# A two-layer hybrid decoder step on one core: the first layer's gate after its norm, mixers in another order, and half of the experts' down pieces in fp16 halves

## What is computed

```python
for i in range(DEPTH):                                  # 2 layers
    n = rms_norm(h, norm_mix[i])
    z = n @ w_in[i]                                      # 1024 -> 7 x 1024
    xa, ya, xb, g_post, g_pre, m_a, m_b = jnp.split(z, SPLIT_IDX, axis=-1)
    ua, ca_new = causal_dwconv(xa, ca0[i], conv_a_w[i])  # width 4
    ua = ua + conv_a_b[i]
    ha, h_last = rg_lru(ua, ...)                         # gated scan
    out_a = (ha * jax.nn.gelu(ya)) @ w_a_out[i]
    ub, cb_new = causal_dwconv(g_pre * xb, cb0[i], conv_b_w[i])
    out_b = (g_post * ub) @ w_b_out[i]
    merged = jax.nn.sigmoid(m_a) * out_a + jax.nn.sigmoid(m_b) * out_b
    h = h + merged @ w_o[i]
    n2 = rms_norm(h, norm_ffn[i])
    h = h + (swiglu(n2, ...) if i == 0 else moe_swiglu(n2, ...))   # top 2 of 8
    h = h + jax.nn.sigmoid(rms_norm(h, norm_ple[i]) @ w_ple_gate[i]) * (p[i] @ w_ple_proj[i])
return rms_norm(h, final_norm), ...
```

## Time and profile before

| what | value |
|---|---|
| median of 3 runs | 1177.38 us (1176.94 to 1178.35) |
| the profiled execution's own time | 1176.44 us |
| its span, and mean granted TensorE clock | 1174.8 us, 0.995 |
| read from HBM | 286.53 MB, 245 GB/s over the span |

### The profile page before, as it was taken

One profiled execution on the slowest core, in us unless ns is written; L12 is line 12 of the kernel. 1 busy time (PEld: TensorE's weight loads), 2 busy tenths in 40 slices (PEclk: granted clock), 3 DMA queues, 4 the chain that ended last, 5 costly groups with the idle time before them and its releaser, 6 DMA issues.

```text
span 1174.8 us, 27209 instructions
## 1 busy us (share of the span) xinstructions
PE 1139.4 (97%) x11871; PEld 919.3 (78%) x11871; DVE 872.5 (74%) x975; ACT 651.7 (55%) x681; POOL 26.8 (2%) x60
## 2 busy tenths in 40 slices
PE   7899999999999999889999998999999999999996
PEld 5788888888888888778888885877777777776565
DVE  5996896779766667896988677977676676767455
ACT  5575644466545457576564446855465555555252
POOL 4000001000000001000001000000000000000000
PEclk9999999999999999999999999999999999999998
DMA  9665566555665654356566654999999999998601
GB/s 284 198 226 180 187 209 215 181 186 171 218 211 181 212 183 143 127 187 223 177 227 228 218 214 178 401 408 396 380 392 382 375 386 379 397 388 320 245 1 39
DMA packets 171069, 289.33 MB, mean 246 GB/s; under 512 B 5195, under 2 KB 132187, under 8 KB 170954
## 3 DMA queue, kind: packets, MB, share of 16 engines
q1 hardware_dynamic: 169040, 283.20, 67.7%
q0 software_dynamic: 1728, 4.16, 1.3%
q10 hardware_dynamic: 202, 0.51, 0.2%
HBM read 286.53 MB, written 1.52 MB: 245 GB/s over the span
## 4 chain that ended last, share of the span: by engine, by line
PE 88%; DVE 7%; ACT 3%; issue 1%; DMA 1%; ACTq 0%; SPq 0%; DVEq 0%
PE acc L572 15%; PE acc L574 15%; PE acc L573 15%; PE aux L916 12%; PE acc L902 5%; PE acc L901 5%; PE acc L903 5%; PE aux L937 2%; PE acc L558 1%; PE acc L564 1%; PE acc L557 1%; PE aux L846 1%; DVE wl L1596 1%; PE aux L750 1%; PE aux L729 1%
## 5 line engine op out<-in xcount | busy, mean ns | idle before, releaser
L1596 DVE SCALAR_TENSOR_TENSOR wl<-raw,wh 128x2048 f16<-128x2048 f32 x124 | 283.3, 2288 | 87.0 <-ACT wh L1092 86.6
L572 PE MATMUL acc<-xn,wh 128*128 128x264 f16 x1184 | 326.8, 276 | 7.6 <-ACT xa L1136 5.0
L574 PE MATMUL acc<-xn,wl 128*128 128x264 f16 x1184 | 326.8, 276 | 0.0
L573 PE MATMUL acc<-xn,wh 128*128 128x264 f16 x1184 | 326.8, 276 | 0.0
L1092 ACT ACTIVATE wh<-raw 128x2048 f16<-128x2048 f32 x124 | 235.6, 1902 | 2.2 <-DMA raw<-in_w_in 2.2
L902 PE MATMUL acc<-ga,wh 128*128 128x96 f16 x1536 | 199.4, 206 | 1.3 <-issue 1.3
L901 PE MATMUL acc<-ga,wh 128*128 128x96 f16 x1536 | 199.4, 206 | 0.0
L903 PE MATMUL acc<-ga,wl 128*128 128x96 f16 x1536 | 199.4, 206 | 0.0
L1602 DVE SCALAR_TENSOR_TENSOR wl<-raw,wh 128x2048 f16<-128x2048 f32 x64 | 144.2, 2287 | 59.4 <-ACT wh L1101 59.4
L1101 ACT ACTIVATE wh<-raw 128x2048 f16<-128x2048 f32 x64 | 121.9, 1910 | 100.1 <-PE acc L903 96.3
L902 PEld LDWEIGHTS acc<-ga,wh 128*128 128x128 f16 x1536 | 150.3, 98 | 7.8 <-issue 7.6
(11 more groups left out here) (334 smaller groups left out, 1807.1 us busy)
## 6 DMA issues: line engine op xcount, KB each, us to landing
raw<-in_moe_w_gu SPq DMA_DIRECT2D x64, 1024.0 KB, 10.0
raw<-in_w_in SPq DMA_DIRECT2D x56, 1024.0 KB, 5.1
raw<-in_ffn_w_gu SPq DMA_DIRECT2D x24, 1024.0 KB, 5.3
sa<-in_moe_w_gu SPq DMA_DIRECT2D x16, 1024.0 KB, 9.3
xb<-in_moe_w_gu SPq DMA_DIRECT2D x16, 1024.0 KB, 10.7
raw<-in_ffn_w_dn SPq DMA_DIRECT2D x12, 1024.0 KB, 4.9
ya<-in_moe_w_dn SPq DMA_DIRECT2D x10, 1024.0 KB, 7.5
sg<-in_moe_w_dn SPq DMA_DIRECT2D x10, 1024.0 KB, 7.5
```

Of the source, the lines that this page charges most:

```text
L572: nc.tensor.matmul(bank, hi, x[:, 0, x0 + k, :], start=(k == 0), stop=False)
L573: nc.tensor.matmul(bank, hi, x[:, 1, x0 + k, :], start=False, stop=False)
L574: last = nc.tensor.matmul(bank, lo, x[:, 0, x0 + k, :], start=False, stop=(k == k_chunks - 1))
L1596: op(V.scalar_tensor_tensor(out=wl[:, s, 0:size], in0=raw_slot[s][:, 0:size], scalar=WS, in1=wh[:, s, 0:size], op0=ALU.mult, op1=ALU.subtr ...
```

## The change

1. **Down pieces.** For experts 0 to 6, pieces 1, 3 and 5 (21 of 48) are split like other weights: ScalarE rounds the loaded piece into `dn_h` (`hi_dn`), VectorE writes the remainder (`lo_dn`), both in `side`, the buffer of the block-diagonal gate weights, which has room for one piece. VectorE also splits two chunks of `hid_e` into `hid_h` (two operations). TensorE makes 12 fp16 matmuls of 512 columns in place of 4 in fp32. The loads that reuse such a piece's slot wait for `dn_lo`. The scale moves into `csr`. The embedding projection's weights of layer 1 go into `side` too, and are loaded by POOL only after the last split piece.
2. **Gate of layer 0** (`ple_mid`). It is a matrix on the normalised `xn`: TensorE sums the squares (four matmuls), projects, then multiplies; ScalarE takes the tanh out of PSUM. The gate of layer 1 (`ple_end`) stays early. All early matrices use `ga`.
3. **Mixers.** The last early unit's remainder of mixer 0 goes behind the four steps of 1/rms; ScalarE evacuates units 2 and 3 ahead of taps and roundings; the convolution of unit u-1 stands behind the scaling of unit u; one operation of the GELU is dropped into the next and into the scale of the tanh.

The core of the diff:

```diff
@@ -43,6 +43,9 @@
+SPLIT_DN = (1, 3, 5)
+
 IN_SECTIONS = 7
...
@@ -191,6 +195,18 @@
         spill_g, spill_t, spill_u, spill_w = (w1_flat[:, at + i * CAP:at + (i + 1) * CAP] for i in range(4))
+        hid_h = w1_flat[:, at:at + 2 * EC // 2 * CAP // 2].bitcast(F16).rearrange("p (s c t) -> p s c t", s=2, c=EC // 2)
+        dn_h = side[:].rearrange("p a c n -> p (a c n)").bitcast(F16).rearrange("p (s n) -> p s n", s=2)
+        def split_down(i):
+            e, g = i // DN_U, i % DN_U
+            return e < NE - 1 and g in SPLIT_DN
...
@@ -341,6 +358,8 @@
                     sp.wait_ge(g_lo, GU_ALL)
+                elif split_down(i - D_SLOTS):
+                    sp.wait_ge(dn_lo, splits(i - D_SLOTS) + 1)
                 else:
...
@@ -490,6 +515,8 @@
             nc.gpsimd.memset(nt[:, :, 2, :], 0.0).then_inc(nt_clear, 1)
+            pool.wait_ge(dn_mm, (NE - 1) * DN_U)
+            project_weights(LAYERS - 1)
             pool.wait_ge(aux_done, AX_POS)
...
-            def ple(l, n, done=0):
-                projected(l, range(done, C))
-                early_stats()
-                if l:
-                    pe.wait_ge(sc_done, C)
-                early_matrix(n, HX_PLE[l], before_norm=True)
             mixer(0)
-            early_matrix(N_GU, HX_FFN, early_stats)
+            early_matrix(N_GU, 1, early_stats)
             pe.wait_ge(xn_ready, 4 * 2)
...
                     unit(N_DN + SEC * k + u, u, u % 2, hid, C, 256, x0=C * k, at=at, last_unit=k == 2 and u == SEC - 1)
-            ple(0, N_PLE[0])
+            norm_stats()
+            projected(0, range(C))
+            matrix(N_PLE[0], xn, xn_ready, 4 * 2, before_norm=True)
...
@@ -906,16 +926,28 @@
                 e, g = i // DN_U, i % DN_U
-                pe.wait_ge(d_loaded[i % D_SLOTS], 16 * (i // D_SLOTS + 1))
-                pe.wait_ge(hid_e_ready, BLOCKS * e + g // 2 + 1)
+                split = split_down(i)
+                if split:
+                    pe.wait_ge(dn_lo, splits(i) + 1)
+                    pe.wait_ge(hid_h_ready, splits(i) + 1)
+                    th, tl = (dn_h[:, s, :].rearrange("p (c m) -> p c m", c=2) for s in range(2))
+                else:
+                    pe.wait_ge(d_loaded[i % D_SLOTS], 16 * (i // D_SLOTS + 1))
+                    pe.wait_ge(hid_e_ready, BLOCKS * e + g // 2 + 1)
+                    w = down_slot(i).rearrange("p (c m) -> p c m", c=2)
                 if g == 0 and e:
                     pe.wait_ge(ys_ready, 2 * e)
-                w = down_slot(i).rearrange("p (c m) -> p c m", c=2)
                 end = g == DN_U - 1
                 for half, k in [(h, k) for h in range(2) for k in range(2)] if end else [(h, k) for k in range(2) for h in range(2)]:
-                    last = nc.tensor.matmul(aux[0:CAP, 2 + half, :], hid_e[:, 2 * g + k, :],
-                                            w[:, k, half * 512:(half + 1) * 512], start=(2 * g + k == 0),
-                                            stop=(2 * g + k == EC - 1))
+                    bank, ms = aux[0:CAP, 2 + half, :], slice(half * 512, (half + 1) * 512)
+                    first, stop = 2 * g + k == 0, 2 * g + k == EC - 1
+                    if split:
+                        x = hid_h[:, :, g // 2 * 2 + k, :]
+                        nc.tensor.matmul(bank, x[:, 0, :], th[:, k, ms], start=first, stop=False)
+                        nc.tensor.matmul(bank, x[:, 0, :], tl[:, k, ms], start=False, stop=False)
+                        last = nc.tensor.matmul(bank, x[:, 1, :], th[:, k, ms], start=False, stop=stop)
+                    else:
+                        last = nc.tensor.matmul(bank, hid_e[:, 2 * g + k, :], w[:, k, ms], start=first, stop=stop)
                     if end and half == 0 and k == 1:
...
@@ -1099,6 +1134,14 @@
                 nc.scalar.activation(wh[:, j % SLOTS, :], g_slot[j % G_SLOTS], ACT.Copy, scale=WS).then_inc(g_hi, 1)
+            def hi_dn(i):
+                act.wait_ge(d_loaded[i % D_SLOTS], 16 * (i // D_SLOTS + 1))
+                k = splits(i)
+                if k:
+                    act.wait_ge(dn_mm, max(j for j in range(i) if split_down(j)) + 1)
+                nc.scalar.activation(dn_h[:, 0, :], d_slot[i % D_SLOTS], ACT.Copy, scale=WS).then_inc(dn_hi, 1)
...
@@ -1259,17 +1300,19 @@
                         hi(n0 + LEAD)
+                    elif u < 2:
+                        hi(n0 + u + LEAD)
+                        if u == l == 1:
+                            stats()
+                        evac(n0 + u, xa[:, 2 * u:2 * u + 2, 3:3 + T])
+                        if u == 1:
+                            norm_hi()
+                            act.wait_ge(aux_done, AX_VEC)
                     else:
+                        evac(n0 + u, xa[:, 2 * u:2 * u + 2, 3:3 + T])
+                        first_tap(u - 2)
                         hi(n0 + u + LEAD)
-                    if u == l == 1:
-                        stats()
-                    if u > 0 or l:
-                        evac(n0 + u, xa[:, 2 * u:2 * u + 2, 3:3 + T])
-                    if u == 1:
-                        norm_hi()
-                        act.wait_ge(aux_done, AX_VEC)
-                    if u:
-                        first_tap(u - 1)
+                first_tap(SEC - 2)
                 if l == 0:
...
-            def ple(l, n):
+            def ple_mid(n):
+                stats()
+                projected(range(4))
+                norm_hi()
+                projected(range(4, C))
+                for u in range(SEC):
+                    hi(n + u + LEAD)
+                    if u:
+                        early_pair(u - 1, 1, False)
+                    if u == SEC - 1:
+                        early_last(n + u, 1, False, ACT.Tanh, 0.5 * UNSCALE)
+                    else:
+                        evac_ot(n + u, ACT.Tanh, 0.5 * UNSCALE)
+            def ple_end(n):
...
@@ -1504,6 +1549,8 @@
                         by_token(e + 2)
+                    if e >= 0 and split_down(e * DN_U + g + 1):
+                        hi_dn(e * DN_U + g + 1)
                     if e == NE - 1 and g in (2, 3, 4):
...
@@ -1602,6 +1649,12 @@
+            def lo_dn(i):
+                vec_e.wait_ge(dn_hi, splits(i) + 1)
+                op(V.scalar_tensor_tensor(out=dn_h[:, 1, :], in0=d_slot[i % D_SLOTS], scalar=WS, in1=dn_h[:, 0, :],
+                                          op0=ALU.mult, op1=ALU.subtract), dn_lo)
...
@@ -1814,8 +1863,10 @@
                     lambdas()
-                lo(n0 + LEAD)
-                norm(v("norm_mix", l))
+                    norm(v("norm_mix", l), scaled=lambda: lo(n0 + LEAD))
+                else:
+                    lo(n0 + LEAD)
+                    norm(v("norm_mix", l))
@@ -1823,18 +1874,21 @@
                     op(V.tensor_tensor(xa[:, s, 3:3 + T], xa[:, s, 3:3 + T], by_rstd(), ALU.mult), xa_scaled)
+                    if u:
+                        vec_e.wait_ge(tap_ready, SEC * l + u)
+                        conv(ua, xa, 4, row, bias, u - 1)
                     lo(n + u + 1 + LEAD)
-                    vec_e.wait_ge(tap_ready, SEC * l + u + 1)
-                    conv(ua, xa, 4, row, bias, u)
                 n += SEC
...
                     evacuated(n + u)
-                    op(V.tensor_scalar(gx[:, s, :], gx[:, s, :], 0.044715 * GELU_C, GELU_C, ALU.mult, ALU.add))
-                    settle()
-                    op(V.tensor_tensor(gx[:, s, :], gx[:, s, :], ya[:, s, :], ALU.mult), vec_step if u == SEC - 1 else dv)
+                    op(V.scalar_tensor_tensor(out=gx[:, s, :], in0=gx[:, s, :], scalar=1.0 / GELU_A, in1=ya[:, s, :],
+                                              op0=ALU.add, op1=ALU.mult), vec_step if u == SEC - 1 else dv)
+                    if u == 0:
+                        vec_e.wait_ge(tap_ready, SEC * l + SEC)
+                        conv(ua, xa, 4, row, bias, SEC - 1)
...
+                norm(v("norm_ple"))
+                vec_e.wait_ge(aux_done, AX_PLE[0])
+                for u in range(SEC):
+                    s = slice(2 * u, 2 * u + 2)
+                    if u < SEC - 1:
+                        lo(n + u + LEAD)
+                    if u:
+                        early_pair(u - 1, 1)
+                    if u == SEC - 1:
+                        last_to_early(n + u, gated_add, 1)
+                        lo(n + u + LEAD)
+                        continue
+                    evacuated(n + u)
+                    op(V.scalar_tensor_tensor(out=ya[:, s, :], in0=ot[:, ots[0] % 2], scalar=1.0, in1=ya[:, s, :],
+                                              op0=ALU.add, op1=ALU.mult), ot_free)
+                    ots[0] += 1
+                    settle()
+                    op(V.scalar_tensor_tensor(out=h[:, s, :], in0=ya[:, s, :], scalar=0.5, in1=h[:, s, :],
+                                              op0=ALU.mult, op1=ALU.add), h_ready)
             gates_seen = [0]
...
                     add_to_h(u)
-            ple(0, N_PLE[0])
```

(15 more changed lines are left out.)

223 lines of the change are left out of this document (100 added, 123 removed).

## The result

| | kernel before | the change |
|---|---|---|
| median of four runs on the device (lowest to highest) | 1177.73 us (1176.94 to 1178.35) | 1162.61 us (1162.13 to 1164.05) |
| profiled execution: span, granted clock | 1174.8 us, 0.995 | 1161.3 us, 0.991 |

The ratio is 0.9874, with a 95% interval from 0.9857 to 0.9891: 15 us faster. The forecast of 1157.3 was 5.3 us too low, inside its range of 1149 to 1169.

The account below looks back on a forecast made before the run. TensorE, busy 97% of the span, was taken as the bound. Savings of 13.0 us in the experts, 3.7 in mixer 0 and 3.3 in gate and mixer 1, 20.0 in all, gave 1157.3 us, range 1149 to 1169.

Parts of the forecast that it names:

- Down pieces, 0.85 us each: Experts: 12 fp16 matmuls in 2.62 us replace 4 fp32 in 3.46; 21 pieces save 17.8 us.
- none in the first: First expert turn, which has no scatters: no new waiting of TensorE for VectorE, so 0 us booked.
- a clock under 1.00: Experts: a granted clock below 1.00 was listed as a sign that the forecast was wrong.
- 0.8 us of new waiting on each turn: Seam between experts: TensorE waits for VectorE's late queue in six turns, 4.8 us in all.
- Transfers: nothing booked: Experts: 408 GB/s and some 10 us of reserve cover the shorter turn of 47.6 us; no loss.
- Rival B: Experts: DMA engines become the bound, a turn is 48.9 us, total 1167; chance 0.18.
- Mixer 0, 3.7 saved: Start of layer 0's mixer: new order removes 3.7 of 4.5 us idle on TensorE, 0.8 left.
- Gate: Layer 0's gate: 1.8 us lost to squares, 3.3 us of waiting gone, VectorE 0.3 sooner at the norm.
- one of the signs: Ahead of layer 0's gate: TensorE waiting about a microsecond for the squares would show the forecast right.
- rival C: Gate of layer 0: the norm ahead of it is not covered, up to 6.3 us, total 1163; chance 0.07.
- Mixer 1, 1.5 saved: Start of layer 1's mixer: same new order saves 1.5 of 3.1 us idle on TensorE.
- Rivals A and D: A: VectorE nowhere late, 1150, chance 0.15. D: VectorE's in-order queue breaks in the experts, 1191, chance 0.05.

Follow-up runs that it names:

- experiment 2: The change, but its first split piece (piece 1 of expert 0) stays fp32: 1158.08 us, 0.9838 of the kernel before.
- version 6: The change with its first split piece whole, pairs and one-hots later at the seam, and additions of chunks 4 to 7 earlier: 1150.42 us.
- experiment 9: version 6 with the third product of the split pieces left out, so output incomplete, all transfers and roundings kept: 1147.59 us.
- experiments 1: The change without fp16 halves: all down pieces stay fp32, mixers' order and gates as changed: 1166.83 us, 0.9907 of the kernel before.
- experiment 11: The change without split pieces, mixers' loops in the old order and unit 3's remainder ahead of the norm again: 1173.58 us.
- experiment 7: The change with its first split piece whole and early additions of chunks 4 to 7, pairs and one-hots left at the seam: 1158.65 us.

## Why the prediction was right or wrong

- **Down pieces, 0.85 us each.** Right: 2.59 us a piece by 0.216 us a matmul, against 2.62. 0.87 us each, 18.3 us in all.
- **The first turn: "none in the first".** Wrong, the largest miss. The wait that I had counted, for the additions, is there only where there are scatters, and I took the rest of VectorE's load over from a turn in the middle. In the first turn its row shows it busy without a gap before the piece, and the stretch ahead of it in the kernel before said so already: VectorE 21.82 of 23.90 us busy at 740 to 763.9. I had read that row for its 408 GB/s alone. Shown by experiment 2: 5.4 us in the trace, 4.5 by the medians.
- **The clock in the experts.** I named a clock under 1.00 as a sign of error, and priced nothing for it. Of the 6.3 us that the first piece lost against its potential (5.4 and the 0.87 that it was to bring), about 3.0 are the wait and 3.0 the lower clock behind it (2.56 in the piece, which took 5.15 us, the rest in the unit).
- **The seam: "0.8 us of new waiting on each turn".** The mechanism was right (pairs and one-hots ahead, the bank that waits for the additions, a remainder at 13.7 us into the turn; it ended 14.1 us in), the size was not: 1.37 us. I counted the remainder of piece 1 and gave the additions 0.3; set against version 6, TensorE is 1.0 us late once it is through scatters 0 and 1, and 0.4 more behind 2 and 3 and the piece between them (0.3 of it is the wait for the remainder). So the additions cost three times what was booked for them, and the remainder half. Six turns give 3.4 us more than booked.
- **The experts' sum.** 18.3 less 6.3 less 6 x 1.37 = 3.8 us, by the medians 4.2; 13.0 were forecast.
- **Transfers: nothing booked.** Right for the change, by 393 GB/s and no wait for a load. But the reason, 408 at best and 10 us of reserve, holds only down to 46.3 us a turn, as experiment 9 shows. The 47.0 us that the prediction gave for 408 GB/s came from 19.2 MB a turn, taken from the rate; the 18 loads are 18.87 MB, and version 6 runs turns of 46.78. Rival B's share of 1.01 said nothing: the share is 1.03 at 408 and 1.00 at 393.
- **Mixer 0, 3.7 saved.** 4.0 by the marks, 4.2 behind the sums of the squares, and 4.2 by the stretches of experiments 1 and 11. The norm's place and the earlier evacuation together were to bring 2.4 us of it, and the rest of the loop's order 1.3; the norm's place by itself brought 1.8, and the loops 2.4.
- **Gate.** The four matmuls of squares cost 1.7 us (1.8 forecast), though no wait of a microsecond stands ahead of them as one of the signs had it; the wait of 3.3 us is gone, and VectorE comes earlier by 1.0 and not 0.3. No wait for the norm (rival C): TensorE starts the gate's unit at 450.45, right behind the projection.
- **Mixer 1, 1.5 saved.** 2.8 by the marks: 0.3 us is left of its 3.1. I had left 1.6 standing out of caution. Part of that is the gate's (the wait that experiment 11 shows shorter by 1.0), and 1.8 the loops'.
- **In all**: 9 us too much in the experts, 2 to 4 too little in the rest. The errors were of opposite sign, and that the total lies within 0.5% is in part luck: of the 13.0 us forecast for the experts a third came.
- **Rivals A and D.** A's 1150 is what version 6 reaches, but only with its changed orders. D never came near: VectorE is at 42.8 of 48.1 us.

## What to carry to other kernels

When a strictly ordered engine gets more work, look at each place where it meets the bounding engine, and at the first turn of a loop apart from the middle ones: the average room (13 us of idle time in a turn here) said nothing on 1.4 us at the seam and 3 at the start. Where lateness has gathered in a queue, an edit at one meeting point may show nothing, and two together all of it (0.03 and 0.23 us alone here, 1.37 together); try them together before you drop either. And the turn's shortest transfer time is the number to hold a faster loop against, since loads made ahead hide it for some turns.

## What the runs showed of the hardware

- A wait of 3.03 us on a TensorE that had been busy at full speed was followed by 6 us at the lower level (0.57 granted in its stretch); one of 1.4 us in the same place was not (1.00). So this wait cost about twice its length. Shorter waits are not always free, though: in the routing, with none over 1.7 us, the granted clock was 0.92 in the kernel before and 0.93 in experiment 7, but 1.00 in the change and in experiment 2.
- The weights' transfers of one core ran at 408 GB/s and no faster for over 180 us, however short the turns were made.
- Matmuls of 512 fp16 columns with 96 stationary ones follow each other in 0.216 us, so that three of them take 0.65 us against 0.87 for one in fp32.
